# A MoE decoder layer on one core: the residual kept as the start value of one copy of the expert sums, two scatters a pass, plain loads in the tail, and the shared down product moved behind the embedding gates

## What is computed

```python
h = layer_norm(DN_ALPHA * h + mix, ln1_g, ln1_b)
x2 = h.reshape(n * s, D_MODEL)
eidx, gw = route(x2, w_router, router_bias)            # 6 of 64 experts a token
ffn = (swiglu(x2, w_s_gate, w_s_up, w_s_down)          # shared expert
       + routed_experts(x2, eidx, gw, w_e_gate, w_e_up, w_e_down))
ple = jax.nn.sigmoid(h @ w_ple_gate) * (p @ w_ple_proj)  # embedding gates
h = layer_norm(DN_ALPHA * h + ffn + ple, ln2_g, ln2_b)
```

## Time and profile before

| | |
|---|---|
| median of 3 runs | 1457.61 us (1453.63 to 1459.3) |
| profiled execution, its own time | 1451.51 us |
| its span, first to last instruction | 1449.7 us |
| mean granted TensorE clock | 0.945 |
| PE / DVE / ACT / POOL busy | 84% / 32% / 21% / 13% of the span |
| read from HBM, written | 286.52 MB, 31.66 MB |

### The profile page before, as it was taken

One profiled execution on the slowest core, in us unless ns is written; L12 is line 12 of the kernel. 1 busy time (PEld: TensorE's weight loads), 2 busy tenths in 40 slices (PEclk: granted clock), 3 DMA queues, 4 the chain that ended last, 5 costly groups with the idle time before them and its releaser, 6 DMA issues.

```text
span 1449.7 us, 20431 instructions
## 1 busy us (share of the span) xinstructions
PE 1222.6 (84%) x7487; PEld 882.7 (61%) x7488; DVE 471.0 (32%) x1040; ACT 299.9 (21%) x537; POOL 194.8 (13%) x232
## 2 busy tenths in 40 slices
PE   3987777799999999999979888878998689998840
PEld 3985545599999999998969533323443234443320
DVE  3235545322444433356675211111111111111115
ACT  2114434231221222224201111111111111111110
POOL 0200000000000100003322222111222112222121
PEclk7999999799999999999989999999999899999985
DMA  8310101132222253425224699999999999999947
GB/s 241 94 59 30 30 2 29 29 81 66 87 87 87 77 201 103 142 86 196 81 112 181 249 382 400 392 384 387 398 377 382 367 394 376 352 388 391 380 95 171
DMA packets 100149, 303.21 MB, mean 209 GB/s; under 512 B 11482, under 2 KB 62514, under 8 KB 75508
## 3 DMA queue, kind: packets, MB, share of 16 engines
q1 hardware_dynamic: 81280, 257.86, 46.6%
q0 software_dynamic: 14976, 38.05, 10.6%
q10 hardware_dynamic: 3844, 6.65, 1.4%
HBM read 286.52 MB, written 31.66 MB: 219 GB/s over the span
## 4 chain that ended last, share of the span: by engine, by line
PE 38%; DMA 37%; DVE 4%; ACT 2%; issue 2%; DVEq 1%; SPq 0%; POOL 0%; ACTq 0%; POOLq 0%
DMA w_exp<-in_w_e_down_dram 26%; PE proj L940 22%; DMA w_exp<-in_w_e_up_dram 9%; PE proj L1093 3%; PE proj L1224 3%; PE att L1280 2%; DMA res<-expert_sums 2%; PE proj L1296 1%; PE att L1102 1%; PE proj L1177 1%; PE att L1177 1%; PE att L1093 1%; PE proj L1206 1%; PE proj L1158 0%; PE att L1061 0%
## 5 line engine op out<-in xcount | busy, mean ns | idle before, releaser
L1280 PE MATMUL att<-w_exp,xt 128*64 128x512 f32 x1280 | 298.3, 619 | 45.1 <-DMA w_exp<-in_w_e_up_dram 34.9
L1280 PEld LDWEIGHTS att<-w_exp,xt 128*64 128x64 f32 x1280 | 112.0, 143 | 225.4 <-issue 225.4
L940 PE MATMUL proj<-h_hi,w_hi 128*128 128x288 f32 x800 | 178.8, 305 | 6.0 <-DVE w_lo L424 3.6
L940 PE MATMUL proj<-h_hi,w_lo 128*128 128x288 f32 x800 | 173.1, 298 | 0.0
L940 PE MATMUL proj<-h_lo,w_hi 128*128 128x288 f32 x800 | 172.8, 298 | 0.0
L1296 PE MATMUL proj<-w_exp,ht_e 128*64 128x512 f32 x640 | 146.2, 597 | 25.6 <-issue 12.9
L940 PEld LDWEIGHTS proj<-h_hi,w_hi 128*128 128x128 f32 x800 | 129.8, 192 | 19.7 <-issue 19.7
L940 PEld LDWEIGHTS proj<-h_lo,w_hi 128*128 128x128 f32 x800 | 130.5, 191 | 0.0
L940 PEld LDWEIGHTS proj<-h_hi,w_lo 128*128 128x128 f32 x800 | 130.5, 191 | 0.0
L1788 DVE TENSOR_TENSOR sg<-sg,att 128x256 f32<-128x256 f32 x40 | 16.9, 422 | 309.6 <-ACT sg L906 309.6
L424 DVE TENSOR_TENSOR w_lo<-w_raw,w_hi 128x2048 fp32r<-128x2048 f32 x33 | 75.6, 2292 | 102.1 <-ACT w_hi L414 96.8
(11 more groups left out here) (329 smaller groups left out, 1720.9 us busy)
## 6 DMA issues: line engine op xcount, KB each, us to landing
w_exp<-in_w_e_gate_dram SPq DMA_DIRECT2D x64, 1024.0 KB
w_exp<-in_w_e_up_dram SPq DMA_DIRECT2D x64, 1024.0 KB
w_exp<-in_w_e_down_dram SPq DMA_DIRECT2D x64, 1024.0 KB
w_raw<-in_w_in_dram SPq DMA_DIRECT2D x21, 1024.0 KB
w_raw<-in_w_in_dram SPq DMA_DIRECT2D x8, 512.0 KB
w_raw<-in_w_attn_out_dram SPq DMA_DIRECT2D x8, 512.0 KB
w_raw<-in_w_conv_out_dram SPq DMA_DIRECT2D x4, 1024.0 KB
expert_sums<-zero_rows POOLq DMA_DIRECT2D x2, 2048.0 KB, 11.8
```

What stands on the lines that cost most here:

```text
L940: last = nc.tensor.matmul(proj[:, 2 * i + a, 0:HALF], lhs, x[:, c, a * HALF:(a + 1) * HALF], start=(c == 0 and n == 0), stop=(c == KC - 1 ...
L1280: last = nc.tensor.matmul(att[e * SLOT:(e + 1) * SLOT, 0, :], xt[:, c, e * SLOT:(e + 1) * SLOT], gate_up[e][:, c, :, :], start=(c == 0), s ...
```

## The change

- `expert_sums` has one copy of 576 rows, and is not zeroed. Instead POOL stores the finished `res` (residual, shared expert, embedding) there by five DMAs, one for each tile, between gate unit 19's product and the second gather.
- A pass has two scatters. `tabs` is two tables: the first has the indices of rows 0 to 63 and 4096 and more (out of bounds) in the others, the second the other way round. POOL issues the first, waits until it has landed, and issues the second. `y_free` of pass k waits for both of pass k-1.
- In the tail POOL raises `all_in`, and SP loads the five tiles of `expert_sums` plainly into `res`; DVE waits for one load of a tile.
- PE makes units 0 to 9 in one go, then tables and units 10 to 14 in turn, units 15 to 19, the ten down products, and `turn(0)`. The high part of the shared activation is made by ACT ahead of unit 15's sigmoid, the low part by DVE behind `routed`; DVE adds `ppo` first (`ppo_added`), then the down products. GpSimd makes all four low parts of the gate weights (before, DVE made the last).
- SP loads gate weights 2 and 3 behind units 4 and 9. Pair 0's down parts go behind pair 2's parts 0 to 3, and the down parts of pairs 1 and 2 wait for `ppo_added`.
- Some buffers are placed elsewhere, since their neighbours in time have changed.

```diff
@@ constants and tables
-    sum_row = np.where(row[:, None] < SLOT, 0, T).astype(np.float32)
+    second_half = np.where(row[:, None] < SLOT, 0, OUT_OF_RANGE).astype(np.float32)
-            nc.vector.tensor_scalar(tabs[:, :], tab_s[:, :], sum_row, -1.0, ALU.add, ALU.add)
+            nc.vector.tensor_scalar(tabs[0][:, :], tab_s[:, :], second_half, -1.0, ALU.add, ALU.add)
+            nc.vector.tensor_scalar(tabs[1][:, :], tab_s[:, :], second_half, OUT_OF_RANGE - 1.0, ALU.subtract, ALU.add)
-        acc_d = nc.dram_tensor("expert_sums", [2 * T, D], F32)
+        acc_d = nc.dram_tensor("expert_sums", [T, D], F32)
@@ SP
-            sp.wait_ge(u_ready, NT)
-            load_gate(2)
-            sp.wait_ge(sd_ready, 2 * NT)
-            for n in range(4, 6):
-                load_part(0, 0, n)
-            sp.wait_ge(u_ready, 2 * NT)
-            load_gate(3)
+            for j in range(2, 4):
+                sp.wait_ge(u_ready, (j - 1) * NT)
+                load_gate(j)
...
-            sp.wait_ge(res_done, 1)
+            sp.wait_ge(sd_ready, 2 * NT)
+            for n in range(4, 6):
+                load_part(0, 0, n)
+
+            sp.wait_ge(ppo_added, NT)
...
+            sp.wait_ge(all_in, 1)
+            for t in range(NT):
+                w = ntok(t)
+                sp.dma_start(res[0:w, t, :], acc_d[t * P:t * P + w, :]).then_inc(summed[t], 16)
@@ POOL
+            for t in range(NT):
+                w = ntok(t)
+                pool.wait_ge(res_done, t + 1)
+                pool.dma_start(acc_d[t * P:t * P + w, :], res[0:w, t, :]).then_inc(scattered, 16)
             pool.wait_ge(xtr, 1)
             gather(1, 1, 2)
...
-                    nc.gpsimd.tensor_copy(sidx_col[i][:, :], tabs[:, bass.ds(k, 1)]).then_inc(idx_ready, 1)
-                    pool.wait_ge(scattered, k * 16 + 32)
+                    nc.gpsimd.tensor_copy(sidx_col[2 * i][:, :], tabs[0][:, bass.ds(k, 1)])
+                    nc.gpsimd.tensor_copy(sidx_col[2 * i + 1][:, :], tabs[1][:, bass.ds(k, 1)]).then_inc(idx_ready, 1)
+                    pool.wait_ge(scattered, k * 32 + 16 * NT)
                     past(nc.gpsimd, 3)
                     nc.gpsimd.sem_inc(y_free, 1)
                     pool.wait_ge(idx_ready, k * 2 + 4)
                     pool.wait_ge(y_a, k + 2)
                     pool.wait_ge(y_dv, k + 2)
                     past(nc.gpsimd, 3)
-                    pool.indirect_dma_start(out=acc_d[:, :], out_offset=bass.IndirectOffsetOnAxis(ap=sidx_col[i][:, 0:1], axis=0),
...
+                    for e in range(2):
+                        if e:
+                            pool.wait_ge(scattered, k * 32 + 16 * NT + 16)
+                            past(nc.gpsimd, 3)
+                        pool.indirect_dma_start(out=acc_d[:, :], in_=ysb[:, i, :], in_offset=None,
+                                                out_offset=bass.IndirectOffsetOnAxis(ap=sidx_col[2 * i + e][:, 0:1], axis=0),
+                                                bounds_check=T - 1, oob_is_err=False, compute_op=ALU.add).then_inc(scattered, 16)
...
+            nc.gpsimd.sem_inc(all_in, 1)
@@ PE
-            for u in range(NT):
-                gate_unit(u)
+            for u in range(2 * NT):
+                gate_unit(u)
+            pe.wait_ge(rank_read, 1)
+            for i in range(NTK // TPAIR // 2):
+                table_products(2 * i)
+                table_products(2 * i + 1)
+                gate_unit(2 * NT + i)
+            for u in range(3 * NT, N_UNITS):
+                gate_unit(u)
...
@@ DVE
+            for t in range(NT):
+                r = res[0:ntok(t), t, :]
+                dve.wait_ge(u_mul, 3 * NT + t + 1)
+                nc.vector.scalar_tensor_tensor(r, r, ALPHA, ppo(t)[0:ntok(t), :], ALU.mult, ALU.add).then_inc(ppo_added, 1)
+            dve.drain()
+            for n, (t, c) in enumerate(QUADS):
...
+                last = nc.vector.tensor_tensor(r, r, sd_bank(n)[0:w, :], ALU.add)
+                last.then_inc(sd_read, 1)
+                if c == 1:
+                    dve.drain().then_inc(res_done, 1)
```

More of the change, by code:

```diff
@@ L325, in decoder_step @@
         gidx_col = [at(f"gidx_col{i}", [P, 1], U32, o_h + 22528 + 512 + 32 * i) for i in range(2)]
-        sidx_col = [at(f"sidx_col{i}", [P, 1], U32, o_h + 22528 + 576 + 32 * i) for i in range(2)]
+        sidx_col = [at(f"sidx_col{i}", [P, 1], U32, o_h + 22528 + 576 + 32 * i) for i in range(4)]
         x2_d = nc.dram_tensor("x2_rows", [T, D], F32)
-        acc_d = nc.dram_tensor("expert_sums", [2 * T, D], F32)
+        acc_d = nc.dram_tensor("expert_sums", [T, D], F32)
         def tile_bank(t):
@@ L372, in decoder_step @@
         summed = [sem(f"summed{t}") for t in range(NT)]
-        acc_zero, zero_ready, y_free = sem("acc_zero"), sem("zero_ready"), sem("y_free")
+        y_free = sem("y_free")
         y_done, y_out = sem("y_done"), sem("y_out")
@@ L634, in _ @@
             gate_low(2)
-            pool.wait_ge(acc_zero, 32)
-            pool.wait_ge(scattered, 32)
-            pool.wait_ge(sd_ready, 2 * NT)
+            for u in range(NT, 2 * NT + 1):
+                ple_product(u)
+            gate_low(3)
+            for u in range(2 * NT + 1, 3 * NT):
+                ple_product(u)
             nc.gpsimd.memset(xg[:, :, :], 0.0).then_inc(x_zero, 1)
-            for u in range(NT, 3 * NT - 2):
-                ple_product(u)
             pool.wait_ge(routed, 1)
@@ L891, in _ @@
                     gate_hi(3)
-                if u == 3 * NT + 3:
-                    xt_half(0)
+                if u == 3 * NT:
+                    act.wait_ge(hs_ready, 2)
+                    nc.scalar.activation(hs_hi[:, :, :], hs_f[:, :, :], ACT.Copy).then_inc(hs_hd, 1)
                 act.wait_ge(u_ready, u + 1)
@@ L1226, in gate_unit, with turn @@
                 last.then_inc(u_ready, 1)
-            for u in range(NT):
+            def turn(k):
+                pe.wait_ge(gathered, k * 16 + 16)
+                for c in range(KC):
+                    last = nc.tensor.transpose(proj[:, c // 4, c % 4 * P:(c % 4 + 1) * P], xg[:, :, c], ident[:, :])
+                last.then_inc(xtr, 1)
+            for u in range(2 * NT):
[5 more added lines that the diff above has]
+                gate_unit(2 * NT + i)
+            for u in range(3 * NT, N_UNITS):
                 gate_unit(u)
@@ L1238, in _ @@
                 wide_products(*sd_w, t, c, hs_hi, hs_lo, sd_bank(n)[0:w, :]).then_inc(sd_ready, 1)
-            def turn(k):
-                pe.wait_ge(gathered, k * 16 + 16)
-                for c in range(KC):
-                    last = nc.tensor.transpose(proj[:, c // 4, c % 4 * P:(c % 4 + 1) * P], xg[:, :, c], ident[:, :])
-                last.then_inc(xtr, 1)
-            gate_unit(NT)
-            gate_unit(NT + 1)
-            pe.wait_ge(rank_read, 1)
-            for i in range(NTK // TPAIR // 2):
-                table_products(2 * i)
-                table_products(2 * i + 1)
-                gate_unit(NT + 2 + i)
-            for u in range(2 * NT + 2, 3 * NT + 3):
-                gate_unit(u)
             pe.wait_ge(routed, 1)
             turn(0)
-            for u in range(3 * NT + 3, N_UNITS):
-                gate_unit(u)
             pe.wait_ge(sd_read, 2 * NT)
@@ L1733, in _ @@
             dve.drain()
-            dve.wait_ge(x2_out, 16 * NT)
-            for n, (t, c) in enumerate(QUADS):
-                w = ntok(t)
-                r = res[0:w, t, c * 512:(c + 1) * 512]
-                dve.wait_ge(sd_ready, n + 1)
-                nc.vector.scalar_tensor_tensor(r, r, ALPHA, sd_bank(n)[0:w, :], ALU.mult, ALU.add).then_inc(sd_read, 1)
             for m in range(NTK // TPAIR):
@@ L1777, in _ @@
             xt_half(0)
-            dve.wait_ge(u_mul, N_UNITS)
-            for t in range(NT):
-                w = ntok(t)
-                last = nc.vector.tensor_tensor(res[0:w, t, :], res[0:w, t, :], ppo(t)[0:w, :], ALU.add)
-            last.then_inc(res_done, 1)
             with dve.Fori(0, half_passes(dve)) as it:
```

61 lines of the change are left out of this document (20 added, 41 removed).

## The result

The changed kernel takes 1624.81 us in the median of 4 runs (1620.92 to 1633.54); the kernel before, on the same chip, 1458.2 us (4 runs, 1453.63 to 1459.3). The ratio is 1.1157, with an interval of 1.1106 to 1.1209. The profiled execution took 1625.38 us, its span 1623.5. The forecast was 1620, between 1530 and 1690, and slower with a chance of 0.91.

A forecast was written before the change was run, and what follows sets the result against it. The prediction took the stream of expert weights as the present bound and two ordered scatter landings a pass as the new one. First `ysb` at 821, loop 753 and tail 42.9 gave a 1617 us span; it said 1620, range 1530 to 1690.

The forecast's parts named there:

- The ring: Expert loop: two scatters in order, each landing before the next step, `ysb` included; 2L + 3.2 us a pass.
- L: Landing time of one half scatter in the expert loop: taken as 8.8 us beside weights, 5.8 without.
- The sign named for this step: In the loop DVE and ACT would wait at `ysb` for POOL's `y_free`, not for PE.
- the other signs: Loop: passes 18 to 21 us apart, DMA share some 0.8 from 820 us on, PE busy about 65%.
- rival B: Loop: half scatters cost as much as whole ones, 10.2 and 6.25 us; 1682 us, inside the forecast's range, no separate chance.
- The rule against the change: Loop scatters: by the skill's swizzle, a half leaves each of its eight engines the whole one's work; L's upper bound would hold.
- Part 1: Stage ahead of the experts: down products move behind unit 19, so the first pass starts 8.5 us earlier.
- the later waits are covered: Ahead of the experts: after a 1.8 us wait at unit 7, PE waits no more; unit 19 ends at 786 us.
- Part 3: Tail, last `ysb` to the end: 42.9 us instead of 50.7, 8 us saved.
- A, short halves: Loop: half scatters land under 5.7 us beside weights, so the weight stream stays the bound; 1432 us, chance 0.07.
- C, the clock: Loop: PE's clock stays at the lower level, a pass takes 26 us; some 1890 us, chance 0.03.
- D: No change to be seen: landings just near 6 us, gains and ring cancel; 1450 to 1530 us, chance 0.06.

The follow-up runs named there:

- experiment 1: Changed kernel with the second half's scatter adding to a second tensor, so no wait between a pass's two scatters; 1454.13 us.
- experiment 3: Changed kernel with each load of an expert weight part fetching 64 KB instead of 1 MiB from the fourth pair on; 1412.3 us.
- experiment 5: Changed kernel with one scatter a pass into two copies again, residual stored in the first, both loaded plainly and added by DVE; 1444.12 us.
- experiment 4: Changed kernel with each scatter naming only the 64 partitions of its half, second-half indices moved by a small load; 1506.75 us.
- experiment 6: Kernel of experiment 5 with the low part of the last gate weights made by DVE behind the tables, not by GpSimd; 1438.19 us.
- experiment 8: Kernel before the change with only the residual stored in the first copy and plain tail loads of both copies, added by DVE; 1454.25 us.
- experiment 7: Kernel of experiment 6 with the five residual stores issued on ACT's queue instead of GpSimd's; 1439.77 us.

## Why the prediction came out right

**The bound.** That the order of two landings, not their bytes, would become the bound was right, and so was its rough size. Shown by experiments 1 (order away: 14.33 us a pass) and 3 (weights away: 13.55).

**The ring.** The form was two landings and an overhead, 2L + 3.2. The two landings are right. The overhead is 2.0, because `ysb` is not in the ring: the last step, "`ysb` of the next pass behind the landing of both", failed, and the section on the kernel before says the same of `y_free` one pass too strictly. PE raises `y_free` once at the start (L1084 of the kernel before), so `ysb` may be written one pass ahead. The changed kernel's timeline shows it (DVE and POOL):

```profile
1011.42 0.75 DVE L1781 TENSOR_SCALAR ysb<-proj,tabw 128x512 f32<-128x512 f32 x1 [7.26 <-PE proj L1285]
...
1012.34 1.55 POOL L681 DMA_INDIRECT expert_sums<-ysb,sidx_col  x1 [10.29 <-DMA expert_sums<-ysb,sidx_col]
...
1023.05 1.60 POOL L681 DMA_INDIRECT expert_sums<-ysb,sidx_col  x1 [6.68 <-issue]
```

The `ysb` of 1011.42 is that of the scatter at 1023.05; it is written before the second scatter of the pass before has even gone out (1012.34). The sign named for this step was wrong too: over 830 to 1580 `ysb` waited for PE and hardly for POOL (waits: us in all, times, longest).

```profile
DVE ysb L1781 <- PE proj L1285: 230.2, 39, 7.3
...
PE proj L1226 <- DMA xg<-x_rows,gidx_col: 161.9, 28, 11.4
```

PE in turn waited for the gather, whose issue stands on POOL behind the wait for the first half and the second scatter. That it follows along was said, and in all but three passes it does; in these the gather itself is on the chain of waits (7.09 us from 1073.55, 9.42 from 1323.94, 8.03 from 1534.68).

Of the other signs, the DMA share came as said (0.79), but single passes are not 18 to 21 us apart: by the first scatters' starts 24 of the 39 distances are 19 to 24.5 us and the other 15 are 10 to 19. PE was busy for 74% of the stretch, not 65%, though it did less work: at the lower granted clock a matmul of its down products (L1285) took 811 ns in the mean, for 597 before.

**L.** Taken were 8.8 beside weights and 5.8 without; in the lines of the section on the result it is 9.5 to 11.1 and 6.0 to 6.3. That is the upper bound, 10.2 and 6.25: half a scatter costs what a whole one does, rival B's premise. Medians from issue to landing say the same: 10.2 us for the 40 whole scatters of experiment 5 and 10.0 for the 80 halves of experiment 1 (which go out in pairs), both beside a full stream. The mean ring is 19.07, so the mean L, with and without weights beside it, is (19.07 - 2.0)/2 = 8.5, where the sum had (773/40 - 3.2)/2 = 8.1 and rival B (838/40 - 3.2)/2 = 8.9. An L too small by 0.4 to 0.5, twice in a ring, and an overhead too large by 1.2 nearly cancelled: 744 us from first to last `ysb` for 753. The forecast was so close partly by luck; with one sign the two errors would have come to some 80 us (39 x (0.9 + 1.2)).

The parts of the sum cancelled once more. The span was forecast as 1617 and is 1623.5: the first `ysb` came 13.7 us later than forecast, the loop was 9 us shorter, the tail 2 us longer. And the sum by its own terms, 1619 and 6 more for the median, is 1625; the 1620 that was said left most of the 6 out. So the 5 us between forecast and median say little of how exact the working was.

**The rule against the change.** A half scatter lands like a whole one, and experiment 4 shows that 2.6 of its 10.3 us go when the other half's slots are not named. By the swizzle rule of the Trainium skill ("DMA: Bandwidth & Descriptors", "The descriptor swizzle") the half without rows has engines of its own, and a half scatter would take as long as a whole one. The trace agrees as far as the landing time goes; of the share of each engine no view here tells. By the Trainium skill's "Anatomy of one DMA" on the same page half a scatter would be 2.4 us, an estimate. The trace disagrees: 6.0 to 11.1 were measured.

**Part 1.** The forecast was a first pass 8.5 us earlier; it came 5.1 later. The down products were sized right (13.69 us for 14), as was their place. Three steps failed. The first is "the later waits are covered": unit 19 ended at 793.66, not 786. `wj` was there at 744.7 as said, but DVE has to build the tables from it, and PE waited 1.4 us for the first, at 750.79. And GpSimd's low part for the fourth block now falls on the tables: PE waited 2.6 us at 762.12 and 1.2 at 764.50, and its granted clock was 0.81 from 762 to 771. Experiment 6 shows this hold-up, 4.7 of the 7.7 us. `wj` itself was held up by the low part before, which GpSimd made from 739.37 to 743.97; the same product took 0.19 us in experiment 8:

```profile
740.50 3.52 DVE L1714 TENSOR_TENSOR wj<-wj,ssum 128x30 f32<-128x30 f32 x1
```

The second step: the gather was said to go 8 us earlier too; it went at 810.03 behind the stores, for 811.79 before, and its rows were used 14 us later; 4 of these are the stores', by experiment 7. The third: pair 0's down weights, issued behind the down products, landed at 826.75, when PE had just finished `turn` (825.97) (chain of waits of the changed kernel; start, length):

```profile
793.66 13.69 PE att L1098 x60
...
807.74 13.31 DMA w_exp<-in_w_e_down_dram
...
821.07 5.68 DMA w_exp<-in_w_e_down_dram
...
827.09 6.60 PE proj L1285 x16
```

I had noted that they go later, and put it down to the stream, not to the first pass, for which they would be the next wait. The whole miss of part 1 is 13.6 us of a change of 167.

**Part 3.** 44.9 us for a forecast of 42.9. The loads were right (3.52 us for 3.3), the landings 6.20 and 6.04 for 5.8. What was missed is the same step of the ring: the last `ysb` (1578.6) was done ahead of the landing of the pass before, and its first scatter went out 3.6 us behind it (1582.19), not 1.0. DVE started its last stretch at 1599.02 and ended at 1620.21, 21.2 for 21.7.

**The rivals.** A, short halves: no; what it promised of the other parts is there once the second scatter is gone. Its 20 us of parts 1 and 3 are measured as 10 in experiment 5 and 16 in experiment 6. Its 1432 was reckoned from the profiled execution (1451.5 less 20); from the median it would have been 1438, and more with the stalls. C, the clock: the granted clock fell from 0.97 to 0.81 and PE still waited for rows. D: no.

## What to carry to other kernels

When a wait puts two small DMAs of a loop in a row, price their landing beside the traffic that the loop has, not on a quiet chip, and count slots, not rows. Ask of every wait in a ring how many passes back it looks, since a buffer given free at the start takes a whole step out. When work moves to another time, list what runs on GpSimd at that time before calling it covered on DVE.

## What the runs showed of the hardware

- A scatter-add that names 128 slots lands in 10.2 us (median, all of its rows) or 10.0 (median, half of its rows) beside loads that fill the DMA engines, and in 6.0 to 6.3 with nothing beside it, with half of its rows as with all. With no row at all it lands in some 8 and 2.73 us. One that names 64 slots lands in 7.7 and 4.3 to 4.6.
- Slots out of bounds still have packets: 144 for a half, 80 when only its own 64 slots are named, 0.21 MB both times.
- A DVE product of two tiles in SBUF that begins while GpSimd combines two tiles of its own ends only when GpSimd's ends: 4.64 us for 0.44, 3.52 for 0.19. Which instruction is caught changes from kernel to kernel; the one of experiment 6 cost 4.7 us of the path.
- A gather behind 2.36 MB of stores on GpSimd's queue: 13.8 to 14.0 us from its issue to its use; with the stores on ACT's queue 10.05.
